# A gated delta rule in a two-layer network: prepare steps, triangles, query decays and residuals in another order

## The reference, cut to the part that matters

```python
def gdn_chunked(q, k, v, log_a, beta, s0, with_output):
    gam = jnp.cumsum(log_a, axis=-1)
    dec = jnp.exp(jnp.where(incl, gam[..., :, None] - gam[..., None, :], -jnp.inf))
    kk = jnp.einsum('bhncd,bhnsd->bhncs', k, k)
    a_mat = jnp.where(strict, beta[..., :, None] * dec * kk, 0.0) + jnp.eye(GDN_CHUNK)
    uw = lax.linalg.triangular_solve(a_mat, rhs, left_side=True, lower=True, unit_diagonal=True)
    k_dec = k * jnp.exp(gam[..., -1:] - gam)[..., None]
    q_dec = q * jnp.exp(gam)[..., None]
    p = dec * jnp.einsum('bhncd,bhnsd->bhncs', q, k)
    def step(s, inp):
        delta = u_c - jnp.einsum('bhcd,bhde->bhce', w_c, s)
        s_new = gl_c[..., None, None] * s + jnp.einsum('bhcd,bhce->bhde', kd_c, delta)
        o = jnp.einsum('bhcd,bhde->bhce', qd_c, s) + jnp.einsum('bhcs,bhse->bhce', p_c, delta)
```

## Time and profile before

| | us |
|---|---|
| median of 3 runs | 1656.24 (1655.55 to 1656.65) |
| the profiled execution's own time | 1658.45 |
| its span in the trace | 1657.1 |
| PE busy | 1596.1 (96%) |
| DVE busy | 1084.8 (65%) |
| ACT busy | 790.5 (48%) |
| POOL busy | 287.4 (17%) |
| mean granted clock of PE | 0.991 of 2.4 GHz |

### The profile page before, as it was taken

One profiled execution on the slowest core, in us unless ns is written; L12 is line 12 of the kernel. 1 busy time (PEld: TensorE's weight loads), 2 busy tenths in 40 slices (PEclk: granted clock), 3 DMA queues, 4 the chain that ended last, 5 costly groups with the idle time before them and its releaser, 6 DMA issues. The chain is left out here.

```text
span 1657.1 us, 24809 instructions
## 1 busy us (share of the span) xinstructions
PE 1596.1 (96%) x10042; PEld 1405.5 (85%) x10042; DVE 1084.8 (65%) x1483; ACT 790.5 (48%) x1009; POOL 287.4 (17%) x247
## 2 busy tenths in 40 slices
PE   8999999999999998999999999998999899999997
PEld 7878878889987976899988788678998888889986
DVE  5867766588886584677556664364566565668864
ACT  5446555444434553444534453483333554356643
POOL 4754350000010010000004400034575000000000
PEclk9999999999999999999999999998999999999999
DMA  7654341277786350777454323000000265556653
GB/s 257 200 178 153 104 139 64 87 262 249 245 309 213 128 177 26 252 261 230 161 190 141 118 55 102 1 20 1 1 2 1 81 202 178 188 157 201 195 173 115
DMA packets 155392, 240.94 MB, mean 145 GB/s; under 512 B 12272, under 2 KB 80624, under 8 KB 155152
## 3 DMA queue, kind: packets, MB, share of 16 engines
q1 hardware_dynamic: 141632, 208.69, 38.9%
q0 software_dynamic: 6816, 27.08, 4.3%
q10 hardware_dynamic: 6832, 3.59, 0.8%
HBM read 238.29 MB, written 1.05 MB: 144 GB/s over the span
## 5 line engine op out<-in xcount | busy, mean ns | idle before, releaser
L206 DVE TENSOR_TENSOR wlo<-raw,whi 128x2048 fp32r<-128x2048 f32 x200 | 459.8, 2312 | 160.7 <-ACT whi L190 159.6
L190 ACT ACTIVATE whi<-raw 128x2048 fp32r<-128x2048 f32 x198 | 372.7, 1887 | 245.8 <-PE ps L340 162.5
L338 PE MATMUL ps<-xf,whi 128*128 128x256 f32 x1056 | 294.5, 279 | 3.9 <-DVE wlo L206 1.8
L340 PE MATMUL ps<-xf,wlo 128*128 128x256 f32 x1056 | 293.4, 278 | 0.0
L339 PE MATMUL ps<-xf,whi 128*128 128x256 f32 x1056 | 293.4, 278 | 0.0
L338 PE MATMUL ps<-whi,xs 128*128 128x512 f32 x672 | 268.0, 399 | 4.9 <-DVE xs L481 3.5
L340 PE MATMUL ps<-whi,xs 128*128 128x512 f32 x672 | 262.9, 391 | 0.0
L339 PE MATMUL ps<-wlo,xs 128*128 128x512 f32 x672 | 262.4, 390 | 0.0
L338 PEld LDWEIGHTS ps<-xf,whi 128*128 128x128 f32 x1056 | 198.4, 188 | 6.7 <-issue 6.6
L340 PEld LDWEIGHTS ps<-xf,wlo 128*128 128x128 f32 x1056 | 199.2, 189 | 0.0
L339 PEld LDWEIGHTS ps<-xf,whi 128*128 128x128 f32 x1056 | 198.8, 188 | 0.0
(11 more groups left out here) (377 smaller groups left out, 2524.9 us busy)
## 6 DMA issues: line engine op xcount, KB each, us to landing
raw<-in_ffn_w_gate_up SPq DMA_DIRECT2D x88, 512.0 KB, 4.9
raw<-in_a_w_in SPq DMA_DIRECT2D x72, 512.0 KB, 4.5
raw<-in_w_in SPq DMA_DIRECT2D x60, 512.0 KB, 4.5
wide<-in_w_mod POOLq DMA_DIRECT2D x24, 1024.0 KB, 7.3
raw<-in_w_up SPq DMA_DIRECT2D x44, 512.0 KB, 4.6
raw<-in_ffn_w_down SPq DMA_DIRECT2D x40, 512.0 KB, 4.7
raw<-in_b_w_in SPq DMA_DIRECT2D x24, 512.0 KB, 4.6
raw<-in_w_down SPq DMA_DIRECT2D x20, 512.0 KB, 4.1
```

Of the source, the lines that this page charges most:

```text
L190: self.hi_ok.inc(act.activation(self.whi[:, h % NHI, 0:nk, :], self.raw[:, h % NRAW, 0:nk, :], ACT.Copy))
L206: self.lo_ok.inc(dve.tensor_tensor(self.wlo[:, h % NRAW, 0:nk, :], self.raw[:, h % NRAW, 0:nk, :], self.whi[:, h % NHI, 0:nk, :].bitcast(F ...
L338: pe.matmul(o, ahi, bhi, start=start, stop=False)
L340: return pe.matmul(o, alo, bhi, start=False, stop=stop)
```

## The change

Five edits in `gdn_heads`.

1. `early(s)`: groups 4 to 7 begin two rounds later (k = 0 in rounds 2, 7, 12, 17, before it in 0, 5, 10, 15). DVE's `matrices` go from k = 5 to k = 4 and `first` from k = 7 to k = 6, counted from the new start. POOL's `prepare` goes one round later.
2. POOL: in rounds 24 to 27 `last(b)` stands ahead of `right(s)`, before it behind.
3. `Er` becomes two pairs of buffers. The second lies in a slot of 128x2048 that holds weights in other stages. ACT's exponentials of q piece n wait for POOL's multiplies of piece n-2, before it for those of n-1.
4. DVE: the residuals of output steps 0 and 1 move into rounds 48 and 49, behind the write-back and ahead of the triangles of the round; before it they stood behind all triangles.
5. Nothing is added or taken away: every engine has the same instructions.

```diff
             for Gn in range(4, 8):
-                k = s - EVERY * (Gn - 4)
-                if 0 <= k <= EVERY + 2:
+                k = s - EVERY * (Gn - 4) - 2
+                if 0 <= k <= EVERY + 1:
                     out.append((Gn, k))
...
-                    if n:
-                        act.wait_ge(gr_q.sem, n)
+                    if n >= 2:
+                        act.wait_ge(gr_q.sem, n - 1)
...
-                        i_ = act.activation(Er[d], ps[:, 6 + d, :], ACT.Exp)
+                        i_ = act.activation(Er[n % 2][d], ps[:, 6 + d, :], ACT.Exp)
...
-                elif k == EVERY:
+                elif k == EVERY - 1:
                     matrices(Gn)
-                elif k == EVERY + 2:
+                elif k == EVERY + 1:
                     first(Gn)
...
                         gl_x.inc(dve.copy_predicated(XT[ph][:, hs], m4(lev[lv]), split4(ps[:, 4 + q % 2, :])))
+                        if s >= N_ALL:
+                            residuals(s - N_ALL)
                         if ph and lv == len(LEVELS) - 1:
...
+            def residuals(s):
+                n = 8 + s
+                dve.wait_ge(gr_ks.sem, 4 + s + 1)
+                if s >= 2:
+                    dve.wait_ge(gr_xr.sem, n - 1)
...
-                for s in range(10):
+                for s in range(2, 10):
                     if s < 8:
...
+                        residuals(s)
...
+                gs.inc(pool.tensor_tensor(qkv[:, 8 + 2 * n:10 + 2 * n, SEQ:2 * SEQ], q_, Er[n % 2][1].rearrange("p (h n) -> p h n", h=2), ALU.mult))
...
-                if s >= 7 and s % EVERY == 2 and s < 23:
+                if s >= 8 and s % EVERY == 3 and s < N_LS:
                     prepare(3 + s // EVERY)
+                if N_LS <= s < N_LS + 4:
+                    last(s - N_LS)
                 right(s)
                 if s == 4:
                     units(1)
-                if N_LS <= s < N_LS + 4:
-                    last(s - N_LS)
```

More of the change, by code:

```diff
@@ L2294, in build, with gdn_heads @@
     N_LS = 4 * len(LEVELS)
-    def gdn_heads(qkv, G, cols_, masks, o, K, XN, XT, PT, t0, prep, rec, ring, ahead):
+    def gdn_heads(qkv, G, cols_, masks, o, K, XN, XT, PT, t0, prep, rec, ring, spread, ahead):
         g, neg, dd, dk, egl, dif, kl, rq = cols_
@@ L2302, in gdn_heads @@
         R, D1, D2 = rec(512), rec(512), rec(512)
-        Er = [R, D1]
+        Er = [[R, D1], spread]
         U, VT, Y = ring
@@ L2771, in levels @@
                         recurrence(*steps[s - N_LS])
+            def residuals(s):
[3 more added lines that the diff above has]
+                    dve.wait_ge(gr_xr.sem, n - 1)
+                for j, d, h, ph, t, T in chain(n):
+                    i_ = dve.scalar_tensor_tensor(slot(Rl[s % 2], j), slot(ps[:, s % 2, :], j), neg[:, d, h, T:T + 1],
+                                                  tok(2, h, 0, t), ALU.mult, ALU.add)
+                gr_r.inc(i_)
             def outputs():
-                for s in range(10):
+                for s in range(2, 10):
                     if s < 8:
[L2776 to L2783, removed]
+                        residuals(s)
                     q = s - 2
@@ L2850, in recurrence @@
                 q_ = qkv[:, hs, 0:SEQ]
-                gs.inc(pool.tensor_tensor(qkv[:, 8 + 2 * n:10 + 2 * n, SEQ:2 * SEQ], q_, Er[1].rearrange("p (h n) -> p h n", h=2), ALU.mult))
+                gs.inc(pool.tensor_tensor(qkv[:, 8 + 2 * n:10 + 2 * n, SEQ:2 * SEQ], q_, Er[n % 2][1].rearrange("p (h n) -> p h n", h=2), ALU.mult))
                 pool.wait_ge(gs.sem, gs.n)
-                gr_q.inc(pool.tensor_tensor(q_, q_, Er[0].rearrange("p (h n) -> p h n", h=2), ALU.mult))
+                gr_q.inc(pool.tensor_tensor(q_, q_, Er[n % 2][0].rearrange("p (h n) -> p h n", h=2), ALU.mult))
             units(0)
@@ L2907, in layer_c @@
         first = gdn.rearrange("p t n -> p (t n)")[:, 3 * CW:]
-        r1 = slots(hi=0)
+        r1, r2 = slots(hi=0), slots(hi=1)
         ring = (r1(2, CW), slots(1)(4, CW), r1(2, CW))
-        gdn_heads(qkv, G, cols_, masks, gdn, K, XN, XT, PT, first, slots(0), slots(0), ring, z_chunks[0])
+        gdn_heads(qkv, G, cols_, masks, gdn, K, XN, XT, PT, first, slots(0), slots(0), ring, [r2(CW) for _ in range(2)], z_chunks[0])
         c = Carve()
```

## The result

| | us |
|---|---|
| kernel before, median of 4 runs | 1656.45 |
| changed kernel, median of 4 runs | 1641.24 (1639.07 to 1643.53) |
| ratio to the kernel before | 0.9885, 95% interval 0.9858 to 0.9911 |
| profiled execution, its own time | 1641.89, span 1640.6 |
| forecast | 1638.3, range 1634.5 to 1645.0 |

A later session gave the changed kernel 1638.86 (5 runs) at a ratio of 0.9883, interval 0.9862 to 0.9904. The ratio is 19 us, with 4 to either side; the forecast was 17.9. The two medians of the first session lie 15.2 apart, since the median of the changed kernel came out 2.9 above the forecast of 1638.3; the range holds it. The ratios leave out two disturbed executions of several milliseconds in the session of the undone edits (8058.92 with edit 1 undone, 3798.17 of the kernel before).

A forecast was written before the change was run, and what follows sets the result against it. PE, busy for 96% of the span, was taken as the bound, so gains come where it waits or runs slow. 2.3 + 7.6 + 0.6 + 7.4 = 17.9 us off 1656.24 gives 1638.3, range 1634.5 to 1645.

The forecast's parts named there:

- start of the rounds, to the end of round 4: PE runs rounds 1 to 3 before group 4's transposes: 3.9 us less at full clock, net 2.3 after a slow stretch.
- changes of group: Three PE waits of 1.99 us for `matrices` vanish, 6.0, plus one slow stretch of 1.6: 7.6 us gained.
- POOL's triangle: PE's 1.0 us wait for POOL's triangle multiplies shrinks as `last(0)` precedes one `right`: 0.6 gained, a few tenths may remain.
- q, residuals and their slow stretch: At the end of the rounds, `kd` ends 7.4 us earlier, including q's 1.75 and a 2.4 slow stretch.
- the slack of 2.6: In the group changes, DVE's next mask is ready 2.6 us before the following round's inner product on PE needs it.
- q buffers: At the third q row sums, a second buffer pair lets ACT go on at once: PE gains 1.75 us.
- Residuals: At the first output steps, PE's wait for the first residual goes; a new 0.95 us wait for the second appears.
- The rival of POOL and DVE: POOL's q multiplies slow DVE's triangles in rounds 46 to 48, 1.9 us per pair; time 1640.2 or 1641.8; chance 0.20.
- Nothing of the gain is given back: Behind the stage PE is the bound again and weight loads come equally earlier, so the 17.9 us gain stays.

The follow-up runs named there:

- the fill experiment: Changed kernel plus four, then two, unread matrix products in PE's idle time before the first inner product: stage 206.7 and 206.3 against 207.8 us; time 1640.18 and 1638.43.

## Why the prediction was right, step by step

| step | forecast | measured |
|---|---|---|
| start of the rounds, to the end of round 4 | 2.3 | 2.4 |
| changes of group | 7.6 | 8.0 |
| POOL's triangle | 0.6 | 0.7 |
| q, residuals and their slow stretch | 7.4 | 7.5 |
| sum in the stage | 17.9 | 18.5 |

The first line is round 4's end counted from the stage's start: 1130.02 - 1095.26 = 34.8 before, 1124.92 - 1092.53 = 32.4 now. The second runs from there to where `xr` is due, the third is the wait of L2456, the last is what remains. The four measured parts add up to 18.5 before rounding.

*Start.* The new idle was forecast as 2.2 with 0.4 close behind and one slow stretch; it was 2.1, 0.2 and one. The stretch had been put at 1.6, from the earlier trace rows; the fill experiment gives 1.5.

*Changes of group.* No wait, as worked out. The argument for that was half wrong: the slack of 2.6 holds for groups 4 to 6 (2.67 measured), and in group 7, where I had let the row sums of a next group stand for cover, it is 0.6. It cost nothing: even there the mask came 0.6 before PE wanted it. Of the 0.4 above the forecast 0.2 is that each wait cost 2.06 from start to start and not the 1.99 of its row. The one slow stretch in the sum was the draw of one trace, since the kernel with edit 1 undone had two: with two, the gain would have been some 1.6 more.

*POOL's triangle.* 0.34 remained; "a few tenths" was forecast, for the reason given: the second multiply took 1.66 in place of 1.27 beside DVE.

*q buffers.* Right in the trace pair. But the price of the wait, without a slow stretch, was one draw: the run with one pair shows the same wait at 4.9. The forecast took a slow stretch into account for the new wait and not for those that went away unless the trace had one. Had that draw fallen the other way in the kernel before, the gain would have been 3.2 more. That the forecast hit this well is to that extent luck.

*Residuals.* No wait for the first, 0.63 for the second where 0.95 was forecast. DVE's residual, triangle pair and write-back followed each other a little more closely than the sum of their lengths.

*The rival of POOL and DVE.* Half of it happened: the pairs of rounds 46 and 47 took 3.0 and 2.4 in place of 1.4. The pair of round 48 took 0.68 and 0.69, since POOL's last multiply ended at 1267.1, ahead of it. (The Trainium skill, SBUF — State Buffer, Who interferes with whom: a DVE operation with two SBUF inputs and a GpSimd one that reads SBUF lock each other out. The trace agrees for the triangles, 1.65 against 0.69, and for the copies with a mask from SBUF, L2723, 1.46 against 0.73; DVE operations that read PSUM kept their 0.67 beside POOL.)

*What failed.* "Nothing of the gain is given back" behind the stage: in this pair of traces 4.7 us were, and 2.7 were gained ahead of it. Ahead of it the instructions are the same too, and the 14 traces begin the stage anywhere from 1092.5 to 1095.9, the changed kernel's two at 1092.5 and 1094.3. The last section shows that the same kernel gave both lengths of that part, so it does not come from the change.

## What to carry to other kernels

Where one engine is the bound, count its waits, and for each find what would be late next: here that sum came within 0.6 us of 18.5. A step whose result is wanted in the same round costs a wait each time; moved one round ahead it costs nothing, as long as the engine's queue behind it has slack, which has to be worked out for the last time round the loop as well as for the others. An idle time of about 2 us on TensorE can cost as much again in clock, and filling it with products that nothing reads took that back. Whether it does can differ from trace to trace (1.7 or 4.9 us for the same wait here), so the price of a wait that is read from one trace holds the draw of that trace.

## What the runs showed of the hardware that was not expected

*The same products at two paces, at full clock.* Outside of the stage the instructions are the same, yet PE ran 256-column products at one of two paces over long stretches. Busy PE and its count over 12 us in the last such stretch, granted clock 1.00 in both, before and then changed:

```profile
1501.60:1513.60 12.00, 12.00 (x108) 12.00 (x107) 9.35 (x14) 7.94 (x11) 0.00 (x0) 1.00 0.67 197
```
```profile
1492.30:1504.30 12.00, 12.00 (x104) 12.00 (x104) 8.91 (x12) 7.50 (x11) 0.00 (x0) 1.00 0.57 180
```

111 ns a product in one, 115 in the other, 4%, over some 110 us: the 4.7 us by which the part behind the stage was longer. In another stretch of the changed kernel's trace the pace went from 91 products in 10 us to 87 in the middle. Of 14 traces, 10 had the last stretch at 90 or more in 10 us and 4 at 87 or 88. The changed kernel is on both sides: behind the stage it took 340.2 us in its first trace and 335.6 in the second. The kernel before has one trace, on the side of the 10. What picks the pace stays open; no run was made for it. It accounts for 4.7 us of difference between traces, and is why the stage and not the time was compared; of runs without a trace it is not known.

*How short an idle time lets the clock fall.* Idle times of 1.0 to 1.4 us were followed by no slow stretch. 1.7 us was in one case of three, 1.98 and 1.99 in three cases of six (one of three in the kernel before, two of three with edit 1 undone). 2.1 was in all seven traces of kernels that have it at the start, which is always the same place. The nine idle times from 2.6 to 4.7 all were. So between 1.7 and 2.0 us the length alone does not decide.
